# Weight slots of a two-stack transformer kernel moved by a few bytes against the operands they are multiplied with

## Time and profile before

| | |
|---|---|
| median of three runs | 3097.29 us (3096.5 to 3097.96) |
| profiled execution, first to last instruction | 3098.1 us |
| TensorE clock granted, mean | 0.998 of full speed |
| TensorE matmul busy | 3057.2 us (99%), 19070 matmuls |
| weight loads busy | 2614.6 us (84%), 19070 |
| VectorE / ScalarE / GpSimd busy | 1979.3 / 1490.0 / 150.2 us |
| DMA | 275.40 MB, mean 89 GB/s, queue q1 at 24.7% of the 16 engines |

### The profile page before, as it was taken

The page is one execution under the profiler, slowest core; times in us unless marked ns, Lnnn a source line. Parts: engine busy times, 40 slices in busy tenths (PEclk is TensorE's granted clock), DMA queues, the critical chain, the costliest instruction groups (busy, mean ns, idle before and its releaser), DMA issues.

```text
span 3098.1 us, 45081 instructions
## 1 busy us (share of the span) xinstructions
PE 3057.2 (99%) x19070; PEld 2614.6 (84%) x19070; DVE 1979.3 (64%) x2723; ACT 1490.0 (48%) x2068; POOL 150.2 (5%) x158
## 2 busy tenths in 40 slices
PE   9999999999999999999999999999999999999999
PEld 7999887888789998989887788789998886888777
DVE  7667449754575765758447855566674568554774
ACT  5444436554443444435335753444344657454673
POOL 0000000300000000000000200000000005000150
PEclk9999999999999999999999999999999999999999
DMA  4232321132122322232221123122323220222202
GB/s 159 96 112 93 120 72 67 43 113 92 69 90 91 113 90 108 87 111 105 95 93 68 55 76 110 61 96 88 110 96 105 82 96 29 72 100 95 82 31 87
DMA packets 49544, 275.40 MB, mean 89 GB/s; under 512 B 5312, under 2 KB 8896, under 8 KB 26304
## 3 DMA queue, kind: packets, MB, share of 16 engines
q1 hardware_dynamic: 49344, 272.53, 24.7%
HBM read 270.41 MB, written 2.10 MB: 88 GB/s over the span
## 4 chain that ended last, share of the span: by engine, by line
PE 89%; DVE 6%; ACT 2%; issue 2%; DMA 0%; DVEq 0%; POOL 0%; SPq 0%; ACTq 0%; POOLq 0%
PE banks L348 59%; PE banks L3365 20%; PE banks L2614 1%; PE banks L2655 1%; ACT weights L2995 1%; DVE weights L3043 1%; PE banks L1684 1%; PE banks L1834 1%; PE banks L1650 0%; ACT slab_hi L316 0%; DVE x_blocks_lo L3611 0%; PE banks L1670 0%; DVE weights_turned L3064 0%; PE banks L1847 0%; PE banks L3748 0%
## 5 line engine op out<-in xcount | busy, mean ns | idle before, releaser
L316 ACT ACTIVATE slab_hi<-slab_raw 128x2048 fp32r<-128x2048 f32 (+2 forms) x210 | 357.3, 1701 | 641.6 <-PE banks L348 616.3
L348 PE MATMUL banks<-x_hi,slab_hi 128*128 128x512 f32 x1536 | 608.0, 396 | 2.8 <-DVE x_lo L435 2.3
L348 PE MATMUL banks<-x_hi,slab_lo 128*128 128x512 f32 x1536 | 598.7, 390 | 0.0
L348 PE MATMUL banks<-x_lo,slab_hi 128*128 128x512 f32 x1536 | 598.7, 390 | 0.0
L323 DVE TENSOR_TENSOR slab_lo<-slab_raw,slab_hi 128x2048 fp32r<-128x2048 f32 (+2 forms) x206 | 416.5, 2022 | 189.5 <-ACT slab_hi L316 189.3
L348 PE MATMUL banks<-hidden_parts,slab_hi 128*128 128x512 f32 x1280 | 394.5, 389 | 0.0
L3365 PE MATMUL banks<-x_blocks_hi,x_area_parts 128*128 128x256 f32 x1616 | 378.3, 283 | 0.0
L348 PEld LDWEIGHTS banks<-x_hi,slab_hi 128*128 128x128 f32 x1536 | 288.8, 188 | 70.2 <-issue 8.9
L348 PEld LDWEIGHTS banks<-x_lo,slab_hi 128*128 128x128 f32 x1536 | 288.9, 188 | 61.3 <-issue 2.9
L348 PEld LDWEIGHTS banks<-x_hi,slab_lo 128*128 128x128 f32 x1536 | 288.7, 188 | 60.8
L3365 PE MATMUL banks<-x_blocks_hi,slab_lo 128*128 128x256 f32 x1024 | 289.7, 283 | 0.0
(11 more groups left out here) (453 smaller groups left out, 5441.8 us busy)
## 6 DMA issues: line engine op xcount, KB each, us to landing
slab_raw<-slabs SPq DMA_DIRECT2D x195, 1024.0 KB, 4.8
slab_raw<-slabs SPq DMA_DIRECT2D x64, 704.0 KB, 4.1
slab_raw<-slabs SPq DMA_DIRECT2D x16, 640.0 KB, 3.9
h<-xT SPq DMA_DIRECT2D x8, 256.0 KB, 5.9
memory<-memT SPq DMA_DIRECT2D x2, 1024.0 KB, 5.3
out<-h SPq DMA_DIRECT2D x7, 256.0 KB, 4.9
constants<-con SPq DMA_DIRECT2D x1, 1412.5 KB, 10.2
slab_raw<-slabs SPq DMA_DIRECT2D x4, 256.0 KB, 4.9
```

The costliest lines, as they stand in the source:

```text
L316: self.nc.scalar.activation(self.wh[:, g % self.HIGHS, 0:w], self.raw[:, g % self.RAWS, 0:w], ACT.Copy).then_inc(self.hi_ready, 1)
L348: mm = self.nc.tensor.matmul(out, left[a], right[c], start=start and n == 0, stop=stop and n == 2)
```

## The change

- Each row of the raw slots becomes 2050 elements (8200 bytes), and the slot is elements 1 to 2048 of it. The three slots begin 4, 12 and 20 bytes past the old residue (of 64 bytes). `slab_lo` lies on them as before.
- Each row of the high slots becomes 2110 elements (8440 bytes), from byte 24640 of the area on, and the slot is elements 4 to 2051. The two slots begin 16 and 8 bytes past the residue.
- The whole area is 41472 bytes in place of 40960. Two constants, `neg_tail` and `neg_ones`, that no other line of the kernel reads, are dropped: 1024 bytes of each partition. What lies between the slots and the constants moves up by 512 bytes, what lies behind the constants moves down by 512, so the residue of every other operand stays the same, of 256 bytes too.
- `wide_weights` names the columns 0 to SLAB, and group 0 of the seven-product stage cuts a piece out of one high slot, since the two slots no longer lie next to each other. Its pieces are the same as before.

No instruction is added or removed, and none changes its place in a list.

```
+    RAW_AT, RAW_ROW = 0, SLAB + 2
+    HIGH_AT, HIGH_ROW = 24640, SLAB + 62
+    SLOTS = 41472
...
-        raw = self.top
-        self.raw = keep("slab_raw", [P, self.RAWS, SLAB])
-        self.wl = self.at("slab_lo", [P, self.RAWS, SLAB], raw, F32R)
-        self.wh = keep("slab_hi", [P, self.HIGHS, SLAB], F32R)
+        raw = self.top + self.RAW_AT
+        self.raw = self.at("slab_raw", [P, self.RAWS, self.RAW_ROW], raw)[:, :, 1:1 + SLAB]
+        self.wl = self.at("slab_lo", [P, self.RAWS, self.RAW_ROW], raw, F32R)[:, :, 1:1 + SLAB]
+        self.wh = self.at("slab_hi", [P, self.HIGHS, self.HIGH_ROW], self.top + self.HIGH_AT, F32R)[:, :, 4:4 + SLAB]
+        self.top += self.SLOTS
...
-                     for a in (self.wh[:, g % self.HIGHS, :], self.wl[:, g % self.RAWS, :]))
+                     for a in (self.wh[:, g % self.HIGHS, 0:SLAB], self.wl[:, g % self.RAWS, 0:SLAB]))
...
-            a = self.high_slots[:, at:at + n, :]
+            return self.k.wh[:, at // 4, at % 4 * S:(at % 4 + n) * S]
```

More of the change, by code:

```diff
@@ L62 @@
                         ("w_f", KC * 8)])
-CON, N_CON = columns([("ident", P), ("cumul", S), ("neg_tail", P), ("neg_ones", P), ("heads64", P),
+CON, N_CON = columns([("ident", P), ("cumul", S), ("heads64", P),
                       ("strict", P), ("levels", LEVELS * P), ("rope", P), ("dilated", TB * P),
@@ L79, in constants @@
     put("cumul", np.concatenate([row <= col, np.ones((P, S - P))], 1))
-    put("neg_tail", -1.0 * (row >= col))
-    put("neg_ones", -1.0)
     put("heads64", row // 64 == col // 64)
@@ L3230, in __init__ @@
         self.spare = {dt: k.at(n, [P, 16, S], k.xa_at, dt) for dt, n in ((F32R, "x_area_parts"), (F32, "x_area"))}
-        self.high_slots = k.wh[:].rearrange("p h (n c) -> p (h n) c", c=S)
         self.fifths = k.at("fifth_product", [P, 2, self.COLS], k.xa_at + 6 * 2048)
```

## The result

The changed kernel takes 3137.68 us (median of 4 runs, 3136.34 to 3139.89), the kernel before 3097.62 beside it (3096.5 to 3099.51). The ratio is 1.0130, with a 95% interval of 1.0115 to 1.0144. The forecast was 3010 us with a range of 2975 to 3120; the time lies outside it, and 9 us above the 3129 of the rival of the broken pattern.

The account below looks back on a forecast made before the run. TensorE's matmul-to-matmul spacing was taken to bound the kernel, not DMAs or splitting. Span 3098.1 - 91 for moved slots + 4 for joins TensorE waits for = 3011 us, 3010 by the median; range 2975 to 3120.

Parts of the forecast that it names:

- the rival of the broken pattern: Alternating residues keep TensorE from settling everywhere in L348: +32 us, 3129 us; chance 0.20.
- the left-over time: Time per matmul beyond streaming its columns: 13.5 ns at L348, 13.3 at L3365; said to depend on both operand reads.
- the price of a slot moved by 4 to 20 bytes: On 11526 slab-reading matmuls, between 121.5 us saved and 32 us lost; taken as 91 us saved.
- the full gain: All 11526 slab-reading matmuls drop to the float32 remainder of 2.9 ns: 121.5 us saved.
- the float32 one: Float32 products at L2614 and L2655, only 2.9 and 2.7 ns left over; taken as nearest model for moved slots.
- the `xa_y` stretch: 240 matmuls, moving operand 128 bytes off the slabs, at 231.5 ns each; set the bound of 4.7 ns more.
- the same amount, whatever the length: At L348 and L3365, 13.5 and 13.3 ns left over, so paid once per matmul and its weight load.
- The reading of the pause: Behind a pause spacings ran 0.24, 0.24, 0.22 us before settling at 226.8 ns; 0.22 was the shortest with a slab.
- Some slots alone escape: Rival: residues work differently; if low slots alone gain, 4002 of 11526 matmuls, 42 us saved, 3055 us; chance 0.20.
- No change: Rival: 13.3 ns is the price of a float32r weight change, whatever the address; 3097 us; chance 0.14.
- What was costed at nothing: DMA, ScalarE and VectorE at addresses that are a multiple of 4 alone, shorter constants, new cuts: 0 us each.
- the prediction's reading that two reads meet in one place of SBUF: Moving-operand and next-weight reads sometimes go to the same place of SBUF and one stands back, causing the left-over time.

## Why the prediction was wrong

- **What bounds the kernel: right.** The spacing of TensorE's matmuls set the time in every run, no other engine took over, and of the 36.5 us between the two spans +40.1 are at L348 and L3365; the -3.6 elsewhere were not followed up. That the left-over time depends on how the two reads stand to each other held too, in each experiment.
- **The term that failed** is the price of a slot moved by 4 to 20 bytes: "I take three quarters of the full gain, 91 us. The row it is nearest to is the float32 one". It was bounded by -10.6 and +4.7 ns for 512 columns and measures +6.6 (233.84 against 227.27), above even the upper bound; for 256 columns at L3365 it was -7.8 for those with a slab and measures -1.4 over all of them. I had set the nearest row by the size of the distance, and called 64 and 128 bytes another kind. The measurement has no such division: 4, 12, 20, 64 and 128 bytes all give 232 to 234, and the high slots, counted as 16 and 8 bytes off, act as 80 and 72: 16 over 0 costs nothing and 80 over 0 costs 6.7 ns. The row to go by was the `xa_y` stretch, the only one that had the same type, the same shape and an unequal place. The float32 row differs in type and in passes, and none of the places tried brings 512 columns of float32r below 226.67, so its small remainder was not to be had.
- **The reading of "the same amount, whatever the length"** The earlier trace rows was a coincidence of distance 0. Alone, 256 columns leave 6.7 ns over at a distance of 64 and 13.3 at 0, and 512 columns the other way round, 20.0 and 13.3: it is not one price for each weight load that a move takes away.
- **The reading of the pause** The earlier trace rows was used on the wrong side. One spacing of 0.22 us was taken as a sign that better ones exist. It was part of the way into the steady step: TensorE alone, with both operands at 0, takes 236, 224, 231, 236, 228, 233 and 231 ns in turn on its way to 226.67, as the kernel before does behind that pause. That step was the best found.
- **The rival "the steady pattern breaks for the worse" was right** in mechanism, place and sign, and in its condition (mean above 227.6). It gave 3129. Its terms were +38.4 and -6.4; measured are +49.8 at 512 columns, and -9.7 at 256 with a further -3.6 elsewhere. It was short because its price came from the `xa_y` row, 231.5 ns, while most places stand at 233.3, and two of the pairs, 72 with 4 and with 20, are worse still (235.6, 237.8). It had 0.20 of the chance.
- **Some slots alone escape** fell: low and high slots each lose when moved alone. Single places do escape the loss (12 for the low weights alone, 226.67 ns), but none gains at 512 columns. **No change** fell as well. The Trainium skill's rule behind it ("TensorE: Matmul & The Clock Gate", section "Step-by-step: what each phase is for"), two independent read ports for the weights and the moving operand, would have the place of the weights without effect; here it moves the same matmuls between 226.67 and 237.8 ns with no other engine at work, so the measurement decides against it.
- **What was costed at nothing was nothing**: DMAs to such addresses (4.8 us), ScalarE and VectorE (1704 and 2023 ns mean at L318 and L325; 1701 and 2022 before), constants and cuts (3097.27 against 3096.67 beside it).
- **The range** failed with the chances: 0.66 rested on a row of another type, and its upper end, set at 3120, cut through the rival it should have held.

What stays open: why the mixed places cost what they do, pair by pair, why the low slots alone cost 1.5 ns more in the kernel than in isolation, and which pauses choose a step. The steady steps are measured; what makes them is not, and neither is the prediction's reading that two reads meet in one place of SBUF.

## What to carry to other kernels

When a stream of matmuls runs at a constant spacing, take it that the spacing may be a step that the stream has locked into, and price a disturbance by the row that shares type and shape with it, whatever its distance looks like. Before moving operands by bytes, measure the places in isolation: a hundred matmuls a case told in one run what the long trace could only hint at. And begin such a case both behind a pause and straight from the work that precedes it in the kernel, since the same addresses gave two different steps.

## What the runs showed of the hardware that was not expected

- Float32r matmuls with a weight load each, high and low parts in turn, mostly settle into steps on a grid: three of them together take a multiple of 6.67 ns. 512 columns: 226.67, 228.9, 231.1, 233.3, 235.6, 237.8; 256 columns: 113.3, 115.6, 117.8, 120.0, 122.2. A few places stand between these in the mean (230.0, 232.0, 118.3).
- What chooses among them is mainly the distance of the weights from the moving operand modulo 256 bytes. It is not all: both operands at 4 differ from both at 0, and 512 columns at 240 stand at 226.67 or 228.3 by whether the low moving operand lies another 256 bytes on. For 256 columns the stream's history counts too. At 64 bytes they stand at 117.8 straight behind a steady stream of 512 columns, and at 113.3 at the beginning of a case or after two matmuls of 128 columns; at 128 bytes at 120.0 straight behind 512 columns and at 118.7 behind a pause.
- The best distance depends on the length: 0 for 512 columns (226.67 against 233.3 at 64; nothing tried was faster), 64 for 256 columns (113.3 against 120.0 at 0). Both operands at 4 bytes are bad for both lengths (237.8 and 122.2).
